# A two-layer hybrid decoder step on one core: a 64-byte gap behind the constants, earlier requests for the ada blocks, and a normalisation whose rest is subtracted tile by tile

## The chip, the cores and the metric

The kernel runs on one core of a Trainium2 chip. The metric is device time in microseconds (us) for one execution; lower is better. Engines are named as in the profile: PE is TensorE (PEld its weight loads), DVE is VectorE, ACT is ScalarE, POOL is GpSimd, SP is SyncE, which issues all the DMAs of this kernel.

## What is computed

One inference step of a trunk of two layers, for a prompt of 512 tokens and 8 samples of 8 tokens, which is 576 tokens (T) of 1024 channels. Each layer, in float32:

```
sh1, sc1, g1, sh2, sc2, g2 = split(silu(c) @ w_ada + b_ada, 6)
h = x * (1 + sc1) + sh1
mix, k, v, conv = mixer(h)          # w_in, dilated attention, conv module, merge, w_out
x = LayerNorm(alpha * x + g1 * mix)
h = x * (1 + sc2) + sh2
x = LayerNorm(alpha * x + g2 * ((silu(h @ w_gate) * (h @ w_up)) @ w_down))
```

The new keys and values and the conv states are outputs too.

## The kernel before, in words

Activations lie channel-major in SBUF: x is 8 tiles of 128 channels by 576 tokens. Each engine has its own program, written out by hand; semaphores order them.

**Units.** Weights come in units of 128 output channels by 1024 inputs (SP, line 350, into one of two `w_raw` buffers). ACT rounds a unit to `w_hi` (line 508) and DVE takes the remainder `w_lo` (line 839), three buffers each. PE forms hi*hi + lo*hi + hi*lo for each of 8 channel tiles and two halves of 288 tokens, so a unit is 48 matmuls (line 1231). A layer has 20 units for w_in (0 to 19), 8 for w_out (20 to 27), 44 for gate and up, 24 for w_down.

**Unit pairs after a normalisation.** The first two units of w_in and of gate/up are done by `products_by_tile` (line 1251): as each channel tile of h arrives, PE does the six matmuls of the first unit for it, and six of the second unit for the tile that is LAG behind.

**ada blocks.** w_ada comes in 96 blocks of 1 MB. Blocks 16 to 23 are used inside units 22 to 25 of layer 0, two in a unit, before its channel tiles 3 and 7 (`ada_quad`, line 1340, four matmuls, recorded as eight), out of a ring of two buffers. SP asks for block n only once block n-2 has been used (line 357). SP works strictly in the order written; `around(l, u)` stands behind the fetch of unit u. In it the ada blocks stand ahead of the two stores `k_d` and `v_d` (lines 428, 431; 1.18 MB each), which belong to u = 25.

**Normalisation.** There are four: in each layer one behind w_out (q = 0) and one behind w_down (q = 1). The mean of tiles 0 to 4 is subtracted early. Behind the last unit: DVE adds the last residual; PE sums the rest of the mean (line 1260); ACT loads the Sqrt table (558), copies the rows of squares (560), squares the last tile (549) and the rest (563); PE turns rows into columns (1324, 1327); DVE subtracts the rest from tiles (`take_rest`, 959), reduces the columns (969) and takes the reciprocal (972) after ACT's root (565); PE spreads the result over PSUM (1281, recorded as twelve matmuls); DVE multiplies each tile by it (`normalise`, 985). After the first three normalisations ACT scales each tile (520), rounds it to `h_hi` (527), and DVE takes `h_lo` (858), on which `products_by_tile` waits; DVE's program runs two normalised tiles ahead of `h_lo`. After the fourth ACT scales each tile (540) and SP stores y.

Of the kernel before, what the change touches and what calls it, by code (L numbers as in the profile page):

```python
# [21 lines left out]
P = 128  # L22
# [20 lines left out]
ALPHA = (2 * DEPTH) ** 0.25  # L43
SCALE = HD ** -0.5
NEG = -1e30
LAG = 4
HF = 3
MOST = 3.0e38
M_ORDER = [*range(4, 8), *range(4)]
# [53 lines left out]
for _k in range(QB - 1):  # L103
# [17 lines left out]
           c_norm=CT, cz=CT, z_sq=CT, z_rows=1, z_rows_sb=1, p_sq=1, t_sq=1, o_rows=1, o_rows_sb=1, m_var=1, m_sd=1, m_rcol=1,  # L121
           m_spread=2, rstdc_sb=1, m_f=CT, m_hi=2 * CT, m_lo=2 * CT,
           ln_sum=4, ln_mean=2, ln_cent=2 * NCEN, ln_acc=2, ln_sq=2 * NCEN, ln_rows=2, ln_rows_sb=2, ln_rest=2,
           ln_cols=2, ln_var=2, ln_sd=2, ln_rcol=2, ln_rstd=2, a_hi=FT, a_lo=FT, vec_used=1)


class Steps:
# [31 lines left out]
def trunk(nc, xT, cT, ba_d, w_ada, w_mix, w_dn, kc_d, vc_d, st_d, vec_d, rope_d, eye_d, mp_d, msc_d, msn_d,  # L159
          y_d, k_d, v_d, cp_d, cs_d):  # L160
    with ExitStack() as ctx:
        def sb(name, shape, dt=F32, where=ctx):
            return where.enter_context(nc.sbuf_tensor("sb_" + name, shape, dt))
# [22 lines left out]
        w_lo = sb("w_lo", [P, NW, UNIT], F32R)  # L186
        eye = sb("eye", [P, P])
        ones = sb("ones", [P, P])
        rope = sb("rope", [P, 2, T])
        mp = sb("mp", [P, SEQ])  # L190
        msc = sb("msc", [P, PAST])
# [146 lines left out]
        def _(sp):  # L338
# [39 lines left out]
            def around(l, u):  # L378

                if u == 1:  # L380
                    need(sp, s["vec_used"], l)
                    sp.dma_start(vec[:], vec_d[l]).then_inc(s["vec_in"], 16)
                if l == 0:
                    for n, at in IN_QUADS.items():
                        if u == (max(3, IN_QUADS[n - 2] + 5) if n - 2 in IN_QUADS else 1):
                            fetch_quad(n)
                    for n in range(GU_QUAD0, QUADS):
                        at = GU0 + 2 * (n - GU_QUAD0) if n < DN_QUAD0 else DN0 + 3 * ((n - DN_QUAD0) // 2) + 2 * ((n - DN_QUAD0) % 2)
                        if u == at + 2:
                            fetch_quad(n)  # L390
                if u == 4:
                    sp.wait_ge(s["w_used"], l * UL + 1)
                    sp.dma_start(uS[:, :, :, 0:HIST], st_d[l]).then_inc(s["hist"], 16)
                if u == 13:
                    sp.wait_ge(z_free[1], z_taken(l, Z_IN, CT - 1))
                    sp.wait_ge(s["hist_zero"], l + 1)
                    sp.dma_start(cp_d[l], uP[:, :, SEQ:SEQ + HIST]).then_inc(s["cv_st"], 16)
                    sp.wait_ge(s["hist"], nth(l, "hist", 15))
                    sp.dma_start(cs_d[l], uS[:, :, :, NT:NT + HIST]).then_inc(s["cv_st"], 16)
                if u == (14 if l == 0 else 5):  # L400
                    sp.wait_ge(s["ada_used"], 16 if l == 0 else QUADS)
                    fetch_cache(l, "k", 0)
                if u == QKV0 + 9:
                    sp.wait_ge(s["ss_ps"], nth(l, "ss_ps", 0))
                    fetch_cache(l, "v", 0)
                if u == QKV0 + 12:
                    sp.wait_ge(s["os_ps"], nth(l, "os_ps", 0))
                    fetch_cache(l, "k", 1)
                if u == QKV0 + 15:
                    sp.wait_ge(s["ss_ps"], nth(l, "ss_ps", 1))  # L410
                    fetch_cache(l, "v", 1)
                    sp.wait_ge(s["w_used"], l * UL + N_IN)
                    fetch_cache(l, "k", 2)
                    fetch_cache(l, "k", 3)
                if u == QKV0 + 16:
                    sp.wait_ge(s["os_ps"], nth(l, "os_ps", 1))
                    fetch_cache(l, "v", 2)
                    sp.wait_ge(s["ss_ps"], nth(l, "ss_ps", 2))
                    fetch_cache(l, "v", 3)
                if l == 0:  # L420
                    for n, (at, _) in OUT_QUADS.items():
                        if u == at + (2 if n < 18 else 3):
                            if n < 18:
                                sp.wait_ge(s["os_ps"], nth(0, "os_ps", 2))
                            fetch_quad(n)
                if u == QKV0 + 17:
                    sp.wait_ge(s["rope_done"], nth(l, "rope_done", 2 * CT - 1))
                    sp.dma_start(k_d[l], qk[:, CT:2 * CT, :]).then_inc(s["k_st"], 16)
                    for j in range(2):
                        sp.wait_ge(z_free[j], z_taken(l, Z_IN, N_IN // 2 - 1))  # L430
                    sp.dma_start(v_d[l], vT[:]).then_inc(s["v_st"], 16)
# [67 lines left out]
        def _(act):  # L499
# [55 lines left out]

            def norm_last(l, q):

                nc.scalar.preload_act_table(ACT.Sqrt)
                act.wait_ge(s["ln_rows"], nth(l, "ln_rows", q))
                nc.scalar.activation(halves(rows[0:3 * GW, :]), ROWS_PS[0:3 * GW], ACT.Copy).then_inc(s["ln_rows_sb"], 1)  # L560
                squares(l, q, NCEN - 1)
                act.wait_ge(s["ln_sum"], nth(l, "ln_sum", 2 * q + 1))
                nc.scalar.activation(halves(rows[3 * GW:P, :]), REST_PS[3 * GW:P], ACT.Square, scale=1.0 / D).then_inc(s["ln_rest"], 1)
                act.wait_ge(s["ln_var"], nth(l, "ln_var", q))
                nc.scalar.activation(sd_col, var_col, ACT.Sqrt, bias=eps[0:TW]).then_inc(s["ln_sd"], 1)
# [87 lines left out]
            for l in range(DEPTH):  # L653
# [121 lines left out]
                for m in range(KT - 1):  # L775
                    u = OUT0 + m
                    computed(l, u)
                    if l == 0 and u + 1 == 26:
                        ada_copy(2)
                    split(l, u + 3)  # L780
                    if m == KM:

                        act.wait_ge(s["k_st"], 16 * (l + 1))
                        act.wait_ge(s["v_st"], 16 * (l + 1))
                        norm_first(l, 0)
                    if m == KT - 2:
                        for c in range(NCEN - 1):
                            squares(l, 0, c)
                split(l, OUT0 + KT + 2)
                norm_last(l, 0)  # L790
                modulate(l, 1)
# [16 lines left out]
                for m in range(KT):  # L808
                    for r in range(3):
                        u = DN0 + 3 * m + r  # L810
                        if r == 0 and l == 0 and m == 1:
                            ada_copy(5)
                        if r == 2:
                            if m == KM:
                                norm_first(l, 1)
                            if m == KT - 2:
                                for c in range(NCEN - 1):
                                    squares(l, 1, c)
                        if u < UL - 1:
                            split(l, u + 3)  # L820
                norm_last(l, 1)
# [6 lines left out]
        def _(dve):  # L828
# [132 lines left out]
            def norm_last(l, q):  # L961

                for j in range(2):
                    dve.wait_ge(z_free[j], z_taken(l, (Z_OUT, Z_DN)[q], KT // 2 - 1))
                dve.wait_ge(s["ln_rest"], nth(l, "ln_rest", q))
                for k in range(3):
                    take_rest(l, q, k)
                dve.wait_ge(s["ln_cols"], nth(l, "ln_cols", q))
                nc.vector.tensor_reduce(var_col, COLS_PS.rearrange("p (c j) -> p j c", c=2), mybir.AxisListType.X, ALU.add)\
                    .then_inc(s["ln_var"], 1)  # L970
                dve.wait_ge(s["ln_sd"], nth(l, "ln_sd", q))
                nc.vector.reciprocal(rstd_col, sd_col).then_inc(s["ln_rcol"], 1)
                for k in range(3, KT - 1):
                    take_rest(l, q, k)

            def normalise(l, q, k):
                if k == 0:
                    dve.wait_ge(s["ln_rstd"], nth(l, "ln_rstd", q))
                    st.wait(st.n)
                if k == KT - 1:  # L980
                    dve.wait_ge(s["ln_sq"], nth(l, "ln_sq", NCEN * q + NCEN - 1))
                    take_rest(l, q, k)
                    st.wait(st.n)
                xk = halves(x[:, k, :])
                nc.vector.tensor_tensor(xk, xk, RSTD_PS, ALU.mult).then_inc(s["x_hat"], 1)

            def ada_bias(sec):

# [231 lines left out]
        def _(pe):  # L1220
# [53 lines left out]
                    ins = nc.tensor.matmul(dst[:, j:j + 1], rows_sb[:, j * TW:(j + 1) * TW], ones[:, 0:1], start=True, stop=True)  # L1274
                return ins

            def spread(dst, col):

                for j in range(TG):
                    half, o = divmod(j * TW, H)  # L1280
                    ins = nc.tensor.matmul(dst[:, half, o:o + TW], col[:, j:j + 1].to_broadcast([TW, P]), eye[0:TW, 0:TW],  # L1281
                                           start=True, stop=True)
                return ins
# [34 lines left out]
            def norm_last(l, q):  # L1318
# [8 lines left out]
                    ins = nc.tensor.matmul(COLS_PS[:, TG + j:TG + j + 1], rows[:, j * TW:(j + 1) * TW], row_pick, start=True, stop=True)  # L1327
                ins.then_inc(s["ln_cols"], 1)
                pe.wait_ge(s["ln_rcol"], nth(l, "ln_rcol", q))
                spread(RSTD_PS, rstd_col).then_inc(s["ln_rstd"], 1)  # L1330

            def ada_quad(n):

# [470 lines left out]
```

## Time and profile before

| what | us |
|---|---|
| median of 3 runs | 1585.09 (1582.12 to 2086.45) |
| the profiled execution | 1584.71 |
| its span, first to last instruction | 1582.8 |
| PE busy in the span | 1500.7 |
| DVE busy | 766.4 |
| ACT busy | 548.7 |

The span is what the trace shows; the profiled execution's time is 1.9 us more, for what lies around it. Matmuls are pipelined and overlap in their records, so PE's pace is read from the times between starts and not from its busy share. An idle time in square brackets behind a row of the timeline is that of the engine just before the row, with what ended it.

### The profile page before, as it was taken

The page shows a single profiled execution, that of the slowest core. Times are in us where ns is not written, and L with a number is a line of the kernel's source. Part 1 is how long each engine was busy: PE and PEld are TensorE (multiplying, and loading weights), DVE is VectorE, ACT ScalarE, POOL GpSimd, SP SyncE. Part 2 cuts the span into 40 slices and gives each one's busy share as a digit, 9 for nine tenths or more (in the row PEclk, how much of TensorE's full clock was granted, in tenths as well). Part 3 has the DMA queues.
Part 4 walks back from the last instruction along what each step waited for, and adds up shares of the span by engine and source line. Part 5 has one row for each costly group of instructions (what it writes and reads, how often), then busy time and mean ns, then how long its engine had stood idle before and what let it go on. Part 6 is the DMA issues. An engine that isn't in the chain of part 4 may idle for free.

```text
span 1582.8 us, 26321 instructions
## 1 busy us (share of the span) xinstructions
PE 1500.7 (95%) x11456; PEld 1359.0 (86%) x11456; DVE 766.4 (48%) x1207; ACT 548.7 (35%) x862; POOL 84.9 (5%) x104
## 2 busy tenths in 40 slices
PE   5999988889999999999989999889899999999996
PEld 2887766779999999899979977569799999999995
DVE  1798974364232232322347989846633333332233
ACT  3425566134222222211235255662533222221122
POOL 1000000111000000001001000002100000000100
PEclk7999999989999999999999999989899999999998
DMA  9576244623334433332214542514022222222221
GB/s 382 179 170 175 94 188 173 261 79 147 137 143 160 160 149 143 134 112 78 80 56 133 80 123 98 225 78 140 29 92 81 80 81 88 86 77 84 77 71 61
DMA packets 59523, 197.16 MB, mean 125 GB/s; under 512 B 22544, under 2 KB 22928, under 8 KB 48400
## 3 DMA queue, kind: packets, MB, share of 16 engines
q1 hardware_dynamic: 59408, 195.48, 37.1%
q8 instruction: 91, 1.49, 0.4%
q14 instruction: 24, 0.20, 0.0%
HBM read 187.27 MB, written 8.18 MB: 123 GB/s over the span
## 4 chain that ended last, share of the span: by engine, by line
PE 83%; DVE 6%; ACT 5%; DMA 2%; issue 2%; SPq 0%; POOL 0%; ACTq 0%; DVEq 0%; POOLq 0%
PE ps L1231 68%; PE ps L1340 2%; PE ps L1251 2%; PE ps L1609 2%; DVE sb_y L875 2%; DMA sb_x<-xT 1%; PE ps L1373 1%; ACT sb_E L589 1%; PE ps L1260 1%; PE ps L1281 1%; PE ps L1484 1%; DVE sb_h L858 1%; PE ps L1407 1%; DMA sb_ring<-w_ada 1%; PE ps L1396 1%
## 5 line engine op out<-in xcount | busy, mean ns | idle before, releaser
L1231 PE MATMUL ps<-sb_h,sb_w_hi 128*128 128x288 f32 x4224 | 770.2, 299 | 0.0
L1231 PEld LDWEIGHTS ps<-sb_h,sb_w_hi 128*128 128x128 f32 x4224 | 627.5, 189 | 51.8 <-issue 50.8
L1231 PE MATMUL ps<-sb_h,sb_w_lo 128*128 128x288 f32 x2112 | 451.8, 296 | 0.0
L839 DVE TENSOR_TENSOR sb_w_lo<-sb_w_raw,sb_w_hi 128x1024 fp32r<-128x1024 f32 x192 | 234.8, 1224 | 357.5 <-ACT sb_w_hi L508 357.1
L1231 PEld LDWEIGHTS ps<-sb_h,sb_w_lo 128*128 128x128 f32 x2112 | 340.1, 189 | 0.0
L508 ACT ACTIVATE sb_w_hi<-sb_w_raw 128x1024 fp32r<-128x1024 f32 x192 | 202.1, 1053 | 320.1 <-PE ps L1231 305.8
L875 DVE SCALAR_TENSOR_TENSOR sb_y<-sb_uP,sb_vec,sb_y 128x512 f32<-128x512 f32 x240 | 164.9, 744 | 0.5
L1231 PE MATMUL ps<-sb_a_hi,sb_w_hi 128*128 128x288 f32 x704 | 151.8, 297 | 0.0
L1231 PE MATMUL ps<-sb_a_lo,sb_w_hi 128*128 128x288 f32 x704 | 150.8, 296 | 0.0
L1231 PE MATMUL ps<-sb_a_hi,sb_w_lo 128*128 128x288 f32 x704 | 150.7, 296 | 0.0
L803 ACT ACTIVATE sb_a_hi<-sb_af 128x576 fp32r<-128x576 f32 x44 | 30.2, 686 | 266.7 <-DVE sb_af L1185 266.7
L1185 DVE TENSOR_TENSOR sb_af<-ps,sb_gate 128x576 f32<-128x576 f32 x44 | 33.3, 758 | 177.0 <-PE ps L1231 174.7
L1231 PEld LDWEIGHTS ps<-sb_a_hi,sb_w_hi 128*128 128x128 f32 x704 | 113.4, 189 | 3.7 <-issue 3.5
L1231 PEld LDWEIGHTS ps<-sb_a_lo,sb_w_hi 128*128 128x128 f32 x704 | 113.4, 189 | 0.0
L1231 PEld LDWEIGHTS ps<-sb_a_hi,sb_w_lo 128*128 128x128 f32 x704 | 113.4, 189 | 0.0
L798 ACT ACTIVATE sb_gate<-ps 128x576 f32<-128x576 f32 x44 | 28.7, 652 | 159.1 <-PE ps L1231 155.7
L1251 PE MATMUL ps<-sb_h,sb_w_hi 128*128 128x288 f32 x256 | 54.5, 329 | 17.9 <-DVE sb_h L858 17.3
L1251 PEld LDWEIGHTS ps<-sb_h,sb_w_hi 128*128 128x128 f32 x256 | 43.4, 213 | 22.0 <-issue 18.3
L1187 DVE TENSOR_TENSOR sb_a_lo<-sb_af,sb_a_hi 128x576 fp32r<-128x576 f32 x44 | 33.4, 758 | 33.1 <-ACT sb_a_hi L803 33.1
L580 ACT ACTIVATE sb_E<-sb_E,sb_small 128x128 f32<-128x128 f32 (+3 forms) x64 | 35.4, 554 | 38.9 <-DVE sb_small L1019 38.6
L1340 PE MATMUL ps<-sb_ring,sb_c_in 128*32 128x512 f32 x320 | 42.9, 608 | 4.1 <-DMA sb_ring<-w_ada 4.1
L1396 PE MATMUL ps<-sb_eye,sb_E 128*128 128x128 f32 x160 | 28.5, 281 | 13.4 <-ACT sb_PT L598 8.1
(192 smaller groups left out, 1208.6 us busy)
## 6 DMA issues: line engine op xcount, KB each, us to landing
sb_w_raw<-w_mix SPq DMA_DIRECT2D x144, 512.0 KB, 3.5
sb_ring<-w_ada SPq DMA_DIRECT2D x40, 1024.0 KB, 5.8
sb_w_raw<-w_dn SPq DMA_DIRECT2D x32, 512.0 KB, 3.5
sb_ring<-vc_d SPq DMA_DIRECT2D x12, 1024.0 KB, 8.5
sb_big<-w_ada SPq DMA_DIRECT2D x8, 1024.0 KB, 11.9
sb_ring<-kc_d SPq DMA_DIRECT2D x8, 1024.0 KB, 7.5
sb_w_raw<-w_dn SPq DMA_DIRECT2D x16, 384.0 KB, 3.2
sb_cache_a<-kc_d SPq DMA_DIRECT2D x4, 1024.0 KB, 7.4
```

Source lines behind the costliest of these rows:

```text
L508: nc.scalar.activation(w_hi[:, g % NW, :], w_raw[:, g % NR, :], ACT.Copy).then_inc(s["hi_ready"], 1)
L580: nc.scalar.activation(blk, blk, ACT.Exp, bias=nm8[p % 2][:, c:c + 1], scale=-1.0, accum_out=den8[p % 2][:, c:c + 1]).then_inc(s["exp_read ...
L803: nc.scalar.activation(a_hi[:, i], af[:], ACT.Copy).then_inc(s["a_hi"], 1)
L839: nc.vector.tensor_tensor(w_lo[:, g % NW, :], w_raw[:, g % NR, :], w_hi[:, g % NW, :].bitcast(F32), ALU.subtract)\
L875: ins = nc.vector.scalar_tensor_tensor(out=yp, in0=up, scalar=tap, in1=yp, op0=ALU.mult, op1=ALU.add)
L1185: nc.vector.tensor_tensor(halves(af[:]), Z[1], halves(gate[:]), ALU.mult).then_inc(z_free[1], 1)
L1187: nc.vector.tensor_tensor(a_lo[:, i], af[:], a_hi[:, i].bitcast(F32), ALU.subtract).then_inc(s["a_lo"], 1)
L1231: ins = nc.tensor.matmul(z[:, i], a[:, g % NW, w], b[:, k0 + k, i * H:(i + 1) * H], start=first and k == 0 and t == 0, stop=last and k == ...
L1251: ins = nc.tensor.matmul(Z[u][:, i], a[:, j, w], b[:, k, i * H:(i + 1) * H], start=n == 0 and t == 0, stop=n == KT - 1 and t == 2)
L1340: ins = nc.tensor.matmul(ps[j * GW:(j + 1) * GW, ADA_BANK[k], :], c_in[:, kt, :], buf[:, j * 512:(j + 1) * 512], start=kt == 0, stop=kt == ...
L1396: ins = nc.tensor.transpose(ps[:, 6 + j % 2, (q - k) * P:(q - k + 1) * P], E[:, e, o:o + P], eye[:])
L1609: ins = nc.tensor.matmul(Z[u][:, i], a[:, j, w], b[:, k, i * H:(i + 1) * H], start=n == 0 and t == 0, stop=n == KT - 1 and t == 2)
```

## The change

One float tile of 64 bytes per partition that nothing uses is allocated behind `ones`, so that all tiles allocated later start 64 bytes further on. LAG goes from 4 to 2. Blocks 18 to 23 are written one unit earlier in SP's program. In the normalisation ACT's table load moves up, ahead of the last units' work, and the last square comes before the copy of the rows; DVE subtracts the rest from two tiles before the columns (three before), from two more after the reciprocal (four before), and from tiles 4 to 7 each just before its own multiplication (tile 7 alone before); the spread signals after each half, and tile 0 is multiplied in halves.

```diff
-LAG = 4
+LAG = 2
@@ allocations
         ones = sb("ones", [P, P])
+        sb("gap", [P, 16])
@@ around (SP)
-                        if u == at + (2 if n < 18 else 3):
+                        if u == at + 2:
@@ norm_last (ACT); the table load now behind squares() at m == KT - 2
-                nc.scalar.preload_act_table(ACT.Sqrt)
+                squares(l, q, NCEN - 1)
                 act.wait_ge(s["ln_rows"], nth(l, "ln_rows", q))
                 nc.scalar.activation(halves(rows[0:3 * GW, :]), ...)
-                squares(l, q, NCEN - 1)
@@ norm_last (DVE)
-                for k in range(3):
+                for k in range(2):
                     take_rest(l, q, k)
 ...
-                for k in range(3, KT - 1):
+                for k in range(2, 4):
                     take_rest(l, q, k)
             def normalise(l, q, k):
+                if k >= 4:
+                    if k == KT - 1:
+                        dve.wait_ge(s["ln_sq"], ...)
+                    take_rest(l, q, k)
+                st.wait(st.n)
+                xk = halves(x[:, k, :])
                 if k == 0:
-                    dve.wait_ge(s["ln_rstd"], nth(l, "ln_rstd", q))
+                    dve.wait_ge(s["ln_rstd"], nth(l, "ln_rstd", 2 * q))
+                    st.of(nc.vector.tensor_tensor(xk[:, 0], xk[:, 0], RSTD_PS[:, 0], ALU.mult))
+                    dve.wait_ge(s["ln_rstd"], nth(l, "ln_rstd", 2 * q + 1))
+                    ins = nc.vector.tensor_tensor(xk[:, 1], xk[:, 1], RSTD_PS[:, 1], ALU.mult)
                     st.wait(st.n)
 ...
@@ norm_last (PE)
-                spread(RSTD_PS, rstd_col).then_inc(s["ln_rstd"], 1)
+                for i in range(2):
+                    spread(RSTD_PS, rstd_col, range(i * TG // 2, (i + 1) * TG // 2)).then_inc(s["ln_rstd"], 1)
```

The order of the instructions shows two places. DVE, the normalisation behind w_down of layer 0, before; line 959 is the rest, 985 the multiplication, 858 `h_lo`:

```order
427 L959 SCALAR_TENSOR_TENSOR sb_x<-ps,sb_x 128x576 x3
428 L969 TENSOR_REDUCE sb_cols<-ps 96x6
429 L972 RECIPROCAL sb_cols<-sb_cols 96x6
430 L959 SCALAR_TENSOR_TENSOR sb_x<-ps,sb_x 128x576 x4
431 L985 TENSOR_TENSOR sb_x<-sb_x,ps 128x576 x3
432 L858 TENSOR_TENSOR sb_h<-sb_hf,sb_h 128x576
```

The same place in the changed kernel, up to the multiplication of tile 5 (961 is now the rest, 987, 989 and 992 the multiplication, 860 `h_lo`):

```order
432 L961 SCALAR_TENSOR_TENSOR sb_x<-ps,sb_x 128x576 x2
433 L971 TENSOR_REDUCE sb_cols<-ps 96x6
434 L974 RECIPROCAL sb_cols<-sb_cols 96x6
435 L961 SCALAR_TENSOR_TENSOR sb_x<-ps,sb_x 128x576 x2
436 L987 TENSOR_TENSOR sb_x<-sb_x,ps 128x288
437 L989 TENSOR_TENSOR sb_x<-sb_x,ps 128x288
438 L992 TENSOR_TENSOR sb_x<-sb_x,ps 128x576 x2
439 L860 TENSOR_TENSOR sb_h<-sb_hf,sb_h 128x576
440 L992 TENSOR_TENSOR sb_x<-sb_x,ps 128x576
441 L860 TENSOR_TENSOR sb_h<-sb_hf,sb_h 128x576
442 L961 SCALAR_TENSOR_TENSOR sb_x<-ps,sb_x 128x576
443 L992 TENSOR_TENSOR sb_x<-sb_x,ps 128x576
```

Three rests have moved from ahead of the first multiplication to between the multiplications of tiles 4, 5 and 6. SP, units 24 to 27 of layer 0, before; `sb_ring<-w_ada x2` are blocks 16 and 17, then 18 and 19, and so on, and the two stores belong to unit 25:

```order
43 L357 DMA sb_ring<-w_ada 128x2048 x2
44 L350 DMA sb_w_raw<-w_mix 128x1024
45 L428 DMA k_d<-sb_qk 128x2304
46 L431 DMA v_d<-sb_vT 128x2304
47 L350 DMA sb_w_raw<-w_mix 128x1024
48 L357 DMA sb_ring<-w_ada 128x2048 x2
49 L350 DMA sb_w_raw<-w_mix 128x1024
```

The same place in the changed kernel:

```order
43 L358 DMA sb_ring<-w_ada 128x2048 x2
44 L351 DMA sb_w_raw<-w_mix 128x1024
45 L358 DMA sb_ring<-w_ada 128x2048 x2
46 L429 DMA k_d<-sb_qk 128x2304
47 L432 DMA v_d<-sb_vT 128x2304
48 L351 DMA sb_w_raw<-w_mix 128x1024
49 L358 DMA sb_ring<-w_ada 128x2048 x2
```

Blocks 18 and 19 have moved ahead of the two stores and of unit 26's weights.

## Rows read from the trace of the kernel before

**Rows 1.** The page, busy time and share of the span by engine.
```profile
PE 1500.7 (95%) x11456; PEld 1359.0 (86%) x11456; DVE 766.4 (48%) x1207; ACT 548.7 (35%) x862; POOL 84.9 (5%) x104
```
**Rows 2.** Timeline, second normalisation of layer 0: start, us, engine, line, operation.
```profile
819.22 0.68 ACT L549 ACTIVATE sb_sq_h<-sb_x 128x576 f32<-128x576 f32 x1 [2.35 <-DVE sb_x L940]
...
820.32 1.10 PE L1324 MATMUL ps<-sb_small,sb_sq_h 128*96 128x1 f32 x12
...
820.52 0.64 ACT L563 ACTIVATE sb_rows<-ps 32x576 f32<-32x576 f32 x1 [0.61 <-PE ps L1260]
...
821.28 1.16 PE L1327 MATMUL ps<-sb_small,sb_rows 128*96 128x1 f32 x12
821.30 2.08 DVE L959 SCALAR_TENSOR_TENSOR sb_x<-ps,sb_x 128x576 f32<-128x576 f32 x3 [1.34 <-ACT sb_rows L563]
823.31 0.16 DVE L969 TENSOR_REDUCE sb_cols<-ps 96x6 f32<-96x12 f32 x1
...
824.07 2.87 PE L1281 MATMUL ps<-sb_eye,sb_cols 96*128 96x96 f32 x12 [1.63 <-DVE sb_cols L972]
...
826.98 2.08 DVE L985 TENSOR_TENSOR sb_x<-sb_x,ps 128x576 f32<-128x576 f32 x3 [0.34 <-PE ps L1281]
...
829.33 0.76 DVE L858 TENSOR_TENSOR sb_h<-sb_hf,sb_h 128x576 fp32r<-128x576 f32 x1 [0.27 <-ACT sb_h L527]
...
836.46 0.74 DVE L959 SCALAR_TENSOR_TENSOR sb_x<-ps,sb_x 128x576 f32<-128x576 f32 x1
...
837.24 0.75 DVE L985 TENSOR_TENSOR sb_x<-sb_x,ps 128x576 f32<-128x576 f32 x1
837.91 0.75 DVE L858 TENSOR_TENSOR sb_h<-sb_hf,sb_h 128x576 fp32r<-128x576 f32 x1
```
**Rows 3.** Chain that ended last, in order of time: the pair's last stretch on PE.
```profile
838.72 8.25 PE ps L1251 x60
```
**Rows 4.** Timeline, first normalisation of layer 1.
```profile
1118.42 1.28 ACT L558 ACT_TABLE_LOAD   x1
...
1119.36 1.21 PE L1260 MATMUL ps<-sb_x,sb_ones 128*128 128x288 f32 x4
...
1119.71 0.65 ACT L560 ACTIVATE sb_rows<-ps 96x576 f32<-96x576 f32 x1
...
1120.95 0.64 ACT L563 ACTIVATE sb_rows<-ps 32x576 f32<-32x576 f32 x1
```
**Rows 5.** Timeline, last normalisation, at the end of the program.
```profile
1572.46 4.74 DVE L985 TENSOR_TENSOR sb_x<-sb_x,ps 128x576 f32<-128x576 f32 x7 [0.34 <-PE ps L1281]
1573.25 6.31 ACT L540 ACTIVATE sb_x<-sb_x,sb_pend 128x576 f32<-128x576 f32 x8 [3.98 <-DVE sb_x L985]
```
**Rows 6.** Timeline, SP's issues and PE around the ada blocks of layer 0.
```profile
282.92 0.43 SPq L428 DMA_DIRECT2D k_d<-sb_qk  x1
...
286.10 4.56 SPq L357 DMA_DIRECT2D sb_ring<-w_ada  x2
...
297.77 1.37 PE L1340 MATMUL ps<-sb_ring,sb_c_in 128*32 128x512 f32 x8 [4.12 <-DMA sb_ring<-w_ada]
```
**Rows 7.** Blocks 16 to 24: us from issue to landing.
```profile
DMA to landing us min/median/max: 4.8/5.6/11.6
```
**Rows 8.** Chain that ended last: 24 matmuls behind block 18, and behind block 19.
```profile
299.14 4.59 PE ps L1231 x24
303.73 0.99 PE ps L1340 x8
304.73 3.38 PE ps L1231 x24
```
**Rows 9.** Stretches: us, busy by engine, granted PE clock, DMA share, GB/s.
```profile
296.00:298.00 2.00, 0.23 (x4) 0.16 (x8) 0.00 (x0) 0.00 (x0) 0.00 (x0) 1.00 1.01 424
...
300.00:302.00 2.00, 2.00 (x11) 2.00 (x11) 0.00 (x0) 0.00 (x0) 0.00 (x0) 0.55 0.87 258
```
**Rows 10.** Stretches of two unit pairs: first of layer 0 whole, then a beginning.
```profile
34.10:49.80 15.70, 15.49 (x97) 14.97 (x98) 7.71 (x9) 12.02 (x17) 5.87 (x13) 0.84 0.84 280
...
830.20:834.20 4.00, 3.81 (x14) 3.50 (x15) 3.44 (x6) 3.78 (x6) 1.78 (x5) 0.50 0.00 0
```
**Rows 11.** Groups of instructions: line, operation, count, busy us, mean ns.
```profile
L1268 PE MATMUL ps<-sb_sqc,sb_ones 128*32 128x288 f32 x64 | 4.7, 411 | 2.1 <-ACT sb_sqc L733 2.1
...
L1268 PE MATMUL ps<-sb_sqm,sb_ones 128*32 128x288 f32 x32 | 2.8, 418 | 0.0
```

More of the change, by code:

```diff
@@ L123 @@
            ln_sum=4, ln_mean=2, ln_cent=2 * NCEN, ln_acc=2, ln_sq=2 * NCEN, ln_rows=2, ln_rows_sb=2, ln_rest=2,
-           ln_cols=2, ln_var=2, ln_sd=2, ln_rcol=2, ln_rstd=2, a_hi=FT, a_lo=FT, vec_used=1)
+           ln_cols=2, ln_var=2, ln_sd=2, ln_rcol=2, ln_rstd=4, a_hi=FT, a_lo=FT, vec_used=1)
 class Steps:
@@ L788, in _ @@
                             squares(l, 0, c)
+                        nc.scalar.preload_act_table(ACT.Sqrt)
                 split(l, OUT0 + KT + 2)
@@ L818, in _ @@
                                     squares(l, 1, c)
+                                nc.scalar.preload_act_table(ACT.Sqrt)
                         if u < UL - 1:
@@ L972, in norm_last @@
                 nc.vector.reciprocal(rstd_col, sd_col).then_inc(s["ln_rcol"], 1)
-                for k in range(3, KT - 1):
+                for k in range(2, 4):
                     take_rest(l, q, k)
             def normalise(l, q, k):
+                if k >= 4:
+                    if k == KT - 1:
+                        dve.wait_ge(s["ln_sq"], nth(l, "ln_sq", NCEN * q + NCEN - 1))
+                    take_rest(l, q, k)
+                st.wait(st.n)
+                xk = halves(x[:, k, :])
                 if k == 0:
-                    dve.wait_ge(s["ln_rstd"], nth(l, "ln_rstd", q))
+                    dve.wait_ge(s["ln_rstd"], nth(l, "ln_rstd", 2 * q))
+                    st.of(nc.vector.tensor_tensor(xk[:, 0], xk[:, 0], RSTD_PS[:, 0], ALU.mult))
+                    dve.wait_ge(s["ln_rstd"], nth(l, "ln_rstd", 2 * q + 1))
+                    ins = nc.vector.tensor_tensor(xk[:, 1], xk[:, 1], RSTD_PS[:, 1], ALU.mult)
                     st.wait(st.n)
[L980 to L985, printed above, removed]
+                else:
+                    ins = nc.vector.tensor_tensor(xk, xk, RSTD_PS, ALU.mult)
+                ins.then_inc(s["x_hat"], 1)
             def ada_bias(sec):
@@ L1275, in token_cols, with spread @@
                 return ins
-            def spread(dst, col):
-                for j in range(TG):
+            def spread(dst, col, groups=range(TG)):
+                for j in groups:
                     half, o = divmod(j * TW, H)
```

## The prediction

> **What bounds the kernel now.** I read the page first: PE is busy 1500.7 of 1582.8 us [rows 1], so only places where PE stands still, or waits behind others, can give anything back. The chain that ended last and the timeline then show which places the change touches: the stretch around ada block 18, four normalisations, three unit pairs behind them, and the unit pair at the start. Everything else keeps its instructions and its order. All sums are made against the profiled execution, 1584.71 us; the three runs were 1582.12, 1585.09 and one far off, so it lies on the median within half a microsecond.
>
> **The normalisation ahead of a pair.** In layer 0 behind w_down [rows 2], DVE starts three rests at 821.30 and reduces the columns only at 823.31, when the third is through, though PE's last column matmul ends at 821.28 + 1.16 = 822.44. With two rests (0.67 us a piece, since three take 2.08 and one 0.74) DVE is free at about 822.7. But ACT's copy of the rows, 0.65 us [rows 4], now follows the last square, which starts at 819.22 and takes 0.68 [rows 2]; it ends at about 820.5, and the column matmuls that started at 820.32 slip by 0.3, to an end at 822.75. So the reduction comes at about 822.9: 0.4 earlier. Then the spread, 2.87 us, is unchanged, but behind it only half of tile 0 has to be multiplied, some 0.45 instead of 0.72: 0.27 more. Tile 0 is normalised 0.67 earlier.
>
> Where the table load lies on the path more is won. In layer 1 behind w_out it runs from 1118.42 to 1119.70, the copy follows, and ACT starts on the rest at 1120.95, though PE's sum for it ended at 1119.36 + 1.21 = 1120.57 [rows 4]. With the load done earlier, beside the last units' matmuls, where ACT waits for PE anyway, the rest starts at 1120.6; this and the third rest give 0.8, with the half 1.05. Were that cover gone, the load would cost its 1.28. The same normalisation in layer 0 I put between the two, at 0.85.
>
> **The price of it.** Three rests move in between the multiplications of tiles 4, 5 and 6. A rest and the wait for it cost 0.78 there, as tile 7's do before (836.46 to 837.24) [rows 2]: 2.34 us in all. From the start of `h_lo` of tile 0 (829.33) to the end of tile 5's (837.91 + 0.75 = 838.66) DVE has twelve instructions, eleven at 0.67 and that rest, 8.15 us of 9.33. So 1.2 are free; I let 1.0 of them take new work, since the waits for tiles 0 and 1 stay. Tile 5 then comes 1.34 later, less the earlier start.
>
> **LAG.** Before, when tile 5 arrives, PE still has 60 matmuls to do, and does them without a stop in 8.25 us [rows 3]: 0.1375 each. With LAG 2 two tiles of the second unit, 12 matmuls, have been done by then in time that PE spent waiting, and 48 are left: 6.60, so 1.65 less. Behind w_down that makes -1.65 + 1.34 - 0.67 = -0.98; with starts of 1.05 and 0.85 the other two give -1.36 and -1.16. Together **-3.5**. The bounds: -5.5, if all the free time takes rests and PE's low clock at a pair's start (granted 0.50, 1.2 GHz [rows 10]) ends sooner; 0, if DVE's free time takes none of them. The second units' weights are no new wait: both are split before the residual of the last tile.
>
> At the program's start PE is busy in 15.49 of the 15.70 us of its pair [rows 10]; LAG can only win what is idle: **-0.2**.
>
> **The end.** Behind the last normalisation no matmul follows. DVE multiplies eight tiles, seven from 1572.46 on [rows 5], ACT scales them in 6.31, and y goes out behind the last. The three rests are on the path whole: +2.34, less some 0.45 of earlier start (between 0.3 and 0.67), **+1.9**. ACT hides none of it: eight scalings at 0.79 end at 1579.56, no later than DVE's last tile allows.
>
> **The ada blocks.** Block 18 is asked for at 286.10 [rows 6] and lands 11.6 us later, where others take 4.8 to 5.6 [rows 7]. PE stops for it from 293.65 to 297.77. Behind that its clock is granted 0.55, near 1.2 GHz instead of 2.4 [rows 9], and the 24 matmuls that follow take 4.59 against 3.38, the block's own 1.37 against 0.99 [rows 6, 8]. The stop costs 4.12 + 1.21 + 0.38 = 5.7.
>
> The earlier place in SP's program does not make the request much earlier: it waits until block 16 has been used, and that is what released it at 286.1. What changes is what lies ahead of it. Block 18 now goes ahead of the stores (issued from 282.92 before) and lands at about 291.7, in time for 293.65. Block 19 needs block 17 used, 290.25 (the second request of the row of 4.56 us); SP stands still until then, and the stores, unit 26's weights and block 20 stand behind it. Block 19 lands at 295.9, needed at 293.65 + 0.99 + 3.38 = 298.0. Block 20 is wanted at 302.4. Ahead of it from 290.25 on are block 19 (1.05 MB), the stores (2.36) and the weights (0.52), with itself 4.98 MB, at 424 GB/s [rows 9] 11.7 us. Before, the four pieces from the first store to block 18, 3.93 MB, took from 282.92 to 297.7, 14.8 us, 5.5 more than the rate alone; if half to three quarters of that stays, block 20 lands between 304.7 and 306.1. So the stop moves from block 18 to block 20, 302.4 to about 305.6: 3.2 us. I charge the same 1.6 for the clock. **-0.9**, between +0.5 (a stop of 4.6) and -5.7 (none). Unit 26's weights come later too, but are needed only two units on; ACT's wait for the stores, ahead of the mean at unit 25, lies behind their landing.
>
> By the Trainium skill ("DMA: Bandwidth & Descriptors", section "Queues, rings and completion order") each DMA engine takes the descriptors of a ring in order, so that block 20 cannot pass the stores; the 11.6 against 5.6 us agree [rows 7]. By that rule the stop moves, as summed; if a block could pass, the stretch would give 5.7.
>
> **The gap.** No instruction is added. It shifts `h`, `a_hi` and `ring` from a multiple of 128 bytes to 64 past one. The nearest rows are two equal sums on PE, over `sqc` (on a multiple of 128) and `sqm` (96 past one): 411 and 418 ns [rows 11]. The whole difference, 1.7%, would be 25 us of PE's 1500.7 [rows 1], in either direction; but these two stand in different surroundings, so I take **0**.
>
> **Sum.** -3.5 - 0.2 + 1.9 - 0.9 = -2.7: 1582.0 us.
>
> **Rivals.**
> 1. *The stop at the ada blocks goes and does not come back.* For it: block 19 and the stores could run as fast as the 424 GB/s of the row, and then block 20 lands at about 302.8 and PE barely stops. Against it: the 14.8 us for 3.93 MB. It gives 5.7 instead of 0.9: 1577.2.
> 2. *The pairs lose what they win (slower).* With LAG 2 PE does twelve matmuls for a tile, 1.65 us, and tiles 4 to 7 come 2.1 apart (0.67 + 0.67 + 0.78 on DVE), so it stands still between them; if the clock stays at 1.2 GHz for that, each matmul costs 0.13 more (14 took 3.81 us [rows 10], 0.27 each). For it: the row with 0.55 behind a stop. Against it: before, PE also had holes in these stretches and rose. From 21 more slow matmuls, over the three pairs together, the 2.7 are gone; 24 more in each pair cost 9.4: 1591. The Trainium skill ("TensorE: Matmul & The Clock Gate", section "What's actually happening") has it that throttled is the default and activity releases it, which would go this way; the rise within the pairs [rows 10] shows that sparse work was enough.
> 3. *DVE sets the pace, the free time takes nothing:* each tile from 5 on comes 2.34 later less its start, the pairs give 0.5, and the other three terms sum to +0.8: 1585.0. For it: DVE is busy most of that stretch; against it: the 1.2 us counted above.
> 4. *The addresses matter:* 1557 or 1609.
>
> **How the numbers follow.** Forecast (1579.5 to 1584.5) 0.52; rival 1 0.17; rival 2 0.12; rival 3 0.13; rival 4 0.06, halved by sign. The range goes from 1575.5, rival 1 with the better bound of the pairs at half, to 1588, rival 2 with half its price; outside lie rival 4 and half of rival 2, 0.12. About 2%, 31.7 us, is what a measurement of this kernel can tell from no change; only the addresses reach that far, from 2.1% of PE's time on: faster 0.02, slower 0.03, within 0.95.
>
> **What would show it.** No stop at block 18; a stop of about 3 us at block 20, with a granted clock near 0.5 behind it. The reduction of the columns directly behind PE's, not behind a rest. On PE some 48 matmuls without a stop at the end of a pair. The last multiplication 1.9 us later, counted from the last spread. The prediction is wrong if matmuls of equal shape change their pace, if PE waits for `h_lo` of tile 7, or if the y stores no longer follow ACT.

## The result, and the profile after the change

| | before | after |
|---|---|---|
| median | 1584.09 (6 runs, 1581.73 to 1585.09 and one far off at 2086.45) | 1575.12 (6 runs, 1572.60 to 1577.15) |
| ratio, without the run far off | | 0.9944, 95% interval 0.9934 to 0.9955 |
| profiled execution, span | 1582.8 | 1570.8 |
| PE busy | 1500.7 [rows 1] | 1489.6 |

The change takes 9.0 us off, 0.56%, where 2.7 had been forecast: within 2%, but just outside the range of 1575.5 to 1588.0. The profiled execution of after is the fastest of its six, so its trace shows some 3 us more than the medians.

The page of after, busy time of PE:

```profile
PE 1489.6 (95%) x11456; PEld 1348.6 (86%) x11456; DVE 767.1 (49%) x1211; ACT 549.4 (35%) x862; POOL 85.0 (5%) x104
```

PE does the same 11456 matmuls and is busy 11 us less; DVE and ACT are as busy as before. So something happened to the matmuls themselves. The chain that ended last shows it where they follow one another without a stop (start, us, engine, line, count). Before:

```profile
846.97 57.61 PE ps L1231 x432
...
1147.40 369.60 PE ps L1231 x2772
...
1517.97 25.59 PE ps L1231 x192
```

After (line 1231 is now 1239):

```profile
838.03 57.12 PE ps L1239 x432
...
1136.95 366.52 PE ps L1239 x2772
...
1504.44 25.39 PE ps L1239 x192
```

369.60 / 2772 = 133.33 ns a matmul before, 366.52 / 2772 = 132.22 after: 0.83% less, at the full clock in both (granted 1.00 over these stretches). The program has 8448 + 384 + 192 = 9024 matmuls of this shape (lines 1231, 1251 and 1609 before; a third of the units of w_down have 36 and not 48); 1.11 ns on each would be 10.0 us if all ran at the full clock and PE never waited for others.

Where the 12.0 us of the span went, in us, from the starts of the same matmuls in the two traces:

| stretch | before | after | difference |
|---|---|---|---|
| up to the last unit of w_out, layer 0 | 340.72 | 338.24 | -2.48 |
| normalisation and unit pair behind it | 30.32 | 28.21 | -2.11 |
| gate, up, w_down of layer 0 | 446.62 | 443.81 | -2.81 |
| normalisation and pair behind it | 29.01 | 27.47 | -1.54 |
| w_in, attention, w_out of layer 1 | 270.27 | 271.35 | +1.08 |
| normalisation and pair behind it | 30.16 | 27.58 | -2.58 |
| gate, up, w_down of layer 1 | 416.04 | 412.66 | -3.38 |
| last normalisation to the end | 19.68 | 21.50 | +1.82 |

Of the first row's 2.48, 1.2 are there by 279 us, before the ada blocks; between executions that start differs by as much.

### The profile page after: what moved, and what is told of

Read it like the earlier page. It is cut to its first block, busy times and chain, and to the rows that moved or that the text cites. A ratio compares the mean times of both kernels' runs of the same rounds, so it can differ in the third digit from the quotient of the medians.

```text
span 1570.8 us, 26329 instructions
## 1 busy us (share of the span) xinstructions
PE 1489.6 (95%) x11456; PEld 1348.6 (86%) x11456; DVE 767.1 (49%) x1211; ACT 549.4 (35%) x862; POOL 85.0 (5%) x104
## 4 chain that ended last, share of the span: by engine, by line
PE 84%; DVE 8%; ACT 4%; DMA 2%; issue 2%; SPq 0%; POOL 0%; DVEq 0%; ACTq 0%; POOLq 0%
PE ps L1239 69%; PE ps L1349 3%; PE ps L1259 2%; PE ps L1618 2%; DVE sb_y L877 2%; PE ps L1382 1%; DMA sb_x<-xT 1%; ACT sb_E L589 1%; PE ps L1268 1%; DVE sb_x L992 1%; DVE sb_x L961 1%; DVE sb_h L860 1%; PE ps L1493 1%; PE ps L1289 1%; PE ps L1321 1%
```

## Experiments: is it the gap?

**The gap alone.**

```diff
         ones = sb("ones", [P, P])
+        sb("gap", [P, 16])
```

> The kernel before with one line more: 64 bytes left free behind ones, so that everything laid out behind it (h, a_hi, a_lo, the ring of raw blocks) starts 64 bytes past a multiple of 128 bytes. Theory A (where the moving operand starts sets the pace of the matmuls): the long chain row of equal matmuls goes from 133.3 ns a matmul to 132.2 ns, as in the changed kernel, and over about 9000 such matmuls the time falls by 8 to 10 us, to 1575 to 1576 us. Theory B (the pace went with the shorter lead of the blocks, LAG 2 in place of 4, because a split of weights meets the matmuls at another moment): nothing moves here, 133.3 ns and 1584 us. Theory C (the pace differs from run to run): the time stays within 1 us of the kernel before on the same chip, whatever the pace in one profile is.

Ratio 0.9946 (0.9930 to 0.9963), which is -8.5 us (-11.1 to -5.9), nearly the whole gain; the medians, 1576.91 for 1583.53, are 6.6 apart. The chain:

```profile
842.92 57.12 PE ps L1232 x432
...
1141.82 366.52 PE ps L1232 x2772
```

**The change without its gap.**

```diff
-        sb("gap", [P, 16])
```

> The changed kernel without its gap: LAG 2, the ada blocks one unit earlier and the new order in the normalisation stay. Theory A (the gap sets the pace): 133.3 ns a matmul as before, and 1581 to 1582 us, which is what the prediction's sum gives with the gap at nothing. Theory B (LAG sets the pace): 132.2 ns a matmul and 1575 us, as the changed kernel with its gap.

Ratio 0.9990 (0.9980 to 1.0000), so -1.6 us (-3.2 to 0.0). The pace is the old one:

```profile
1140.85 369.60 PE ps L1238 x2772
```

Theory A holds so far: the gap sets the pace, neither LAG nor the execution does; whether it is the streamed operand's own start that counts comes next. The prediction's -2.7 for all the rest lies between -3.2 and 0.0.

## Experiments: which address counts?

**h moves by 64 bytes.** `pend` takes 64 bytes a partition; laid out behind h it leaves the weights and the blocks behind h where they were. Only `vec`, `c_in`, `small`, the ring and what shares h's place move with h.

```diff
-        pend = sb("pend", [P, 2, KT])     # ahead of vec
...
         h = sb("h", [P, KT, 2, T], F32R)
+        pend = sb("pend", [P, 2, KT])
```

> The kernel before with one small constant (pend, 64 bytes a partition) laid out behind h and not in front of it: h starts 64 bytes lower, so 64 past a multiple of 128 bytes, while a_hi, a_lo and the weights stay where they were. Theory M (the start of the moving operand sets the pace): matmuls that stream h at 132.2 ns, those that stream a_hi and a_lo still at 133.3 ns, in the same run; about 6600 of 9000 such matmuls gain, so about 1578 us. Theory D (the gap worked through something else that moved, such as the blocks behind h): all at 133.3 ns, 1584 us.

Ratio 0.9973 (0.9954 to 0.9992). The chain has both paces in one run: 432 matmuls over h, then a stretch that is mostly h, then 192 over a_hi and a_lo:

```profile
844.92 57.12 PE ps L1231 x432
...
1142.69 367.35 PE ps L1231 x2772
1511.01 25.58 PE ps L1231 x192
```

57.12 / 432 is 132.2 ns, 25.58 / 192 is 133.2: the operand that moved changed its pace, the others did not. Of the 2772, the 42 units of gate and up, 2016 matmuls, stream h and 756 stream a_hi and a_lo; 2016 at 132.22 and 756 at 133.33 are 367.35, as measured.

**The weights move by 64 bytes, the streamed operands stay.** The constants laid out between the weights and `pend` move too.

```diff
+        pend = sb("pend", [P, 2, KT])
         w_hi = sb("w_hi", [P, NW, UNIT], F32R)
...
-        pend = sb("pend", [P, 2, KT])     # ahead of vec
```

> The kernel before with pend laid out in front of w_hi: the weights w_hi and w_lo start 64 bytes later, h, a_hi and a_lo stay where they were. Theory M (the start of the moving operand alone): nothing moves, 133.3 ns a matmul, 1584 us. Theory W (what counts is where the moving operand starts against the weights, which are loaded meanwhile): the same 64 bytes between them as with the gap, so 132.2 ns and 1576 us.

Ratio 0.9963 (0.9944 to 0.9982). h, a_hi and a_lo stand where they did, and yet:

```profile
843.15 57.12 PE ps L1231 x432
...
1141.85 366.52 PE ps L1231 x2772
1509.34 25.38 PE ps L1231 x192
```

Theory M falls, theory W holds: what counts is where the streamed operand starts against the weights.

**Everything moves by 64 bytes.**

```diff
+        sb("gap", [P, 16])
         x = sb("x", [P, KT, T])
```

> The kernel before with the 64 bytes left free in front of everything: weights, h, a_hi and a_lo all start 64 bytes later, so their distance from one another is as before. Theory W (the distance of the moving operand's start from the weights' start, within 128 bytes, sets the pace): 133.3 ns a matmul, 1584 us. Theory E (it is enough that either of the two is off a multiple of 128 bytes): 132.2 ns, 1576 us.

Ratio 1.0001 (0.9991 to 1.0011), and the old pace; so being off a multiple of 128 bytes is not what helps:

```profile
845.61 57.61 PE ps L1232 x432
...
1146.04 369.60 PE ps L1232 x2772
```

**h moves by 384 bytes, to a multiple of 512.**

```diff
-        b_ada = sb("b_ada", [P, SECTIONS, KT])     # ahead of pend
...
         h = sb("h", [P, KT, 2, T], F32R)
+        b_ada = sb("b_ada", [P, SECTIONS, KT])
```

> The kernel before with b_ada (384 bytes a partition) laid out behind h: h starts 384 bytes lower, on a multiple of 512 bytes where it was 384 past one; a_hi, a_lo and the weights stay. Theory M128 (only the start within 128 bytes counts): h still at 133.3 ns a matmul, 1584 us. Theory M512 (the start within 256 or 512 bytes counts): the matmuls that stream h change their pace, to either side, those that stream a_hi and a_lo keep 133.3 ns.

Ratio 0.9999 (0.9988 to 1.0011); 432 matmuls over h took what they took before: 384 bytes, three times 128, change nothing. From tile to tile of one run, too, streamed operand and weights are other multiples of 128 bytes apart, so what is left of the distance within 128 bytes is what counts:

```profile
846.85 57.61 PE ps L1231 x432
```

**Other distances.** The gap's size in floats is 8, 4, 12 and 24 in place of 16.

```diff
-        sb("gap", [P, 16])
+        sb("gap", [P, 8])
```

> The kernel before with a gap of 32 bytes in place of 64 behind ones. If any start off a multiple of 128 bytes gives the pace of the gap: 132.2 ns a matmul and 1576 us. If it must be half of 64 or 128 bytes apart: 133.3 ns or another pace, no lower than 131 ns, the commonest single distance of before.

> The kernel before with a gap of 16 bytes: moving operands 16 bytes past the weights' phase. If only a distance of 64 gains (theory H, half of 128): 133.3 ns a matmul, 1584 us. If the distance matters by degree (theory G): a pace between 132.2 and 133.3, or one that is worse than both.

> The kernel before with a gap of 48 bytes. Theory H: 133.3 ns a matmul, 1584 us. Theory G: between 133.3 (the 32 bytes) and 132.2 (the 64 bytes), 1576 to 1584 us.

> The kernel before with a gap of 96 bytes, which is as far from the next multiple of 128 as 32 bytes are from the last. Theory H, and a theory by which the distance counts the same to both sides: 133.3 ns a matmul as with 32 bytes, 1584 us. If only the direction counts (moving operand more than half behind): 132.2 ns, 1576 us.

The chains of 32, 16, 48 and 96 bytes, in this order:

```profile
1145.35 369.60 PE ps L1232 x2772
```
```profile
1148.17 369.60 PE ps L1232 x2772
```
```profile
1141.27 366.52 PE ps L1232 x2772
```
```profile
1144.57 369.60 PE ps L1232 x2772
```

| streamed operand's start minus the weights', within 128 bytes | ns a matmul | ratio of times |
|---|---|---|
| 0 (before) | 133.33 | 1 |
| 16 | 133.33 | 1.0010 (0.9994 to 1.0026) |
| 32 | 133.33 | 1.0006 (0.9990 to 1.0023) |
| 48 | 132.22 | 0.9949 (0.9926 to 0.9971) |
| 64, by the gap | 132.22 | 0.9946 (0.9930 to 0.9963) |
| 64, by the weights | 132.22 | 0.9963 (0.9944 to 0.9982) |
| 96 | 133.33 | 1.0007 (0.9995 to 1.0018) |

There are two paces among these and nothing between; 48 gains as much as 64, so theory H (64 alone) is too narrow and theory G (by degree) is wrong. Where the gain begins between 32 and 48 and where it ends between 64 and 96 was not tried. The paces are means. In the traces' steady stretches the single starts follow patterns: at 0, three come about 131 ns behind the one before and the fourth 140; at 16 and 32, 135 and 132 alternate; at 96 they lie between 129 and 139; at 48 and 64, between 130 and 135. So the slow pace is the same mean by three patterns, not one delay on each matmul.

## Experiments: the other parts

**The ada blocks alone.**

```diff
-                        if u == at + (2 if n < 18 else 3):
+                        if u == at + 2:
```

> The kernel before with the request of the ada blocks from 18 on one unit earlier, alone. By the prediction's term the stop of 4.1 us ahead of block 18 goes, one of about 3 us ahead of block 20 comes, and 24 matmuls behind it lose about 1 us to the clock: -0.9 us, so about 1583.2 us. Rival 1 (no stop is left at all): -5 to -6 us, so 1578 to 1579 us. By the changed kernel's trace, in which the stream of matmuls is 2.4 us early behind block 20 of which 1.2 us came before: about -1.2 us.

Ratio 1.0001 (0.9988 to 1.0015): nothing that can be measured. The stop moved from block 18 to block 20 here as in the change, but was longer (timeline of PE, with its idle time, then the chain):

```profile
304.69 1.93 PE L1340 MATMUL ps<-sb_ring,sb_c_in 128*32 128x512 f32 x8 [3.52 <-DMA sb_ring<-w_ada]
```
```profile
306.63 5.26 PE ps L1231 x24
```

Stop 3.52, slow block 1.93 - 0.99, slow matmuls 5.26 - 3.38: 6.3, against 5.7 before [rows 6, 8]. In the traces of the change, of the change without its gap and of the better version below, the same edit brings the stream 1.3, 1.5 and 1.3 us forward.

**The normalisation alone.** The edits of `norm_last`, `normalise` and the spread; LAG 4, no gap, ada blocks as before.

> The kernel before with the new normalisation alone (table loaded behind the squares, two halves of the spread signalled apart, rest subtracted tile by tile from the fifth on); no gap, LAG 4, ada blocks as before. By the prediction's terms: -1.2, -1.0 and -1.4 us in front of the three unit pairs, a little at the start pair, and +1.9 us at the end, where no matmuls hide the tiles: -1.5 to -2 us in sum, 1582 to 1582.5 us, with the pace of the matmuls at 133.3 ns. If the reordering itself changed the pace: 132.2 ns and 1574 us.

Ratio 1.0020 (1.0009 to 1.0031): slower by 3.2 us, where 1.5 to 2 us faster had been expected. PE's waits in the first pair of layer 0 (sum, times, longest):

```profile
PE ps L1258 <- DVE sb_h L859: 5.7, 5, 3.0
```

Before, and then with LAG 2 alone (the next run), the same wait:

```profile
PE ps L1251 <- DVE sb_h L858: 3.9, 3, 3.3
```
```profile
PE ps L1251 <- DVE sb_h L858: 3.5, 2, 3.3
```

The longest is the wait for tile 0. The pair starts 1.1 us sooner (12.81 us behind the start of the last product, for 13.90), and then PE stands still 2.7 us for tiles that the inserted rests have made late; before it stood 0.6.

**LAG alone.**

```diff
-LAG = 4
+LAG = 2
```

> The kernel before with LAG 2 in place of 4, alone: in the unit pairs PE does twelve matmuls a tile from the third tile on, not from the fifth. The old normalisation hands over its first tile later and the others quickly, and PE stood 0.7 to 1.0 us for the fifth tile and 0.5 us for the seventh. Theory 1 (the shorter lag takes these stops away by itself): about 1 us less in each of the three pairs, 1581 us. Theory 2 (the lag pays only together with the new normalisation, which without it lost what it won): within 1 us of 1584. Sum of parts: the changed kernel without its gap is at 1582 to 1583, and the normalisation alone is at +3, so with the ada blocks at 0 the lag has to give 4 to 5 us in the new normalisation's company.

Ratio 0.9978 (0.9965 to 0.9991): -3.5 us, theory 1. The interval in us from the first to the last matmul of the three pairs, all without the gap (the new normalisation with LAG 2 is the change without its gap):

| | LAG 4 | LAG 2 |
|---|---|---|
| old normalisation | 16.42, 16.43, 16.43 | 15.69, 15.51, 14.98 |
| new normalisation | 17.79, 18.85, 17.80 | 16.19, 16.18, 16.18 |

The new normalisation costs a pair 0.5 to 1.2 us with LAG 2 and 1.4 to 2.4 with LAG 4, and starts it 1.1 to 2.4 us earlier in five of six (the sixth, behind w_down with LAG 2, 0.1 later). Summed over the three pairs of these single traces that is 1.7 us gained with LAG 2 and 0.7 lost with LAG 4. The times without the gap do not show the gain: 0.9990 for the change without its gap, whose end is 1.5 us longer than before, against 0.9978 for LAG 2 alone.

**Gap and LAG 2 alone.** Does the normalisation add anything to them?

```diff
+        sb("gap", [P, 16])
-LAG = 4
+LAG = 2
```

> The kernel before with the gap of 64 bytes and LAG 2 alone; the old normalisation and the ada blocks as before. If the parts add up: 0.9946 by 0.9978 of 1584, which is 1572 us, 3 us under the whole change and level with the version whose end is mended; then the new normalisation and the ada blocks add nothing in sum. If the new normalisation pays in the company of LAG 2 (its pairs ran 1 to 1.5 us shorter than those of LAG 2 alone): 1574 to 1576 us, and the mended version stays in front.

Ratio 0.9965 (0.9953 to 0.9978), median 1577.61: the second theory by its side, if 1.6 us above its numbers. The parts do not add up: beside the gap alone (0.9946) LAG 2 shows no gain. The whole change (0.9944, 0.9934 to 0.9955) is ahead of these two, though the intervals touch; the version below (0.9925) is clear of them. Its pairs are shorter than those of the gap alone (normalisation and pair 28.86, 27.70, 28.52 against 30.09, 28.97, 29.86), 3.8 us in sum, but w_in to w_out of layer 1 took 272.05 against 269.03.

**A better version.** The changed kernel with the rests of the very last normalisation subtracted early again.

```diff
@@ norm_last (DVE)
-                for k in range(2, 4):
+                for k in range(2, KT - 1 if (l, q) == (DEPTH - 1, 1) else 4):
                     take_rest(l, q, k)
@@ normalise
-                    take_rest(l, q, k)
+                    if k == KT - 1 or (l, q) != (DEPTH - 1, 1):
+                        take_rest(l, q, k)
```

> The changed kernel, but in the very last normalisation, behind which no matmul follows, the rests of tiles 4 to 6 are subtracted while PE makes the reciprocal deviation, as in the kernel before. By the prediction's term for the end and the changed kernel's trace, 1.9 to 2.0 us come back: 1573 us. If the end is set by the output's transfer or by ACT: nothing, 1575 us.

Ratio 0.9925 (0.9912 to 0.9938), median 1572.55: below the change's 0.9944, though the intervals touch and the two were measured apart. The timeline of DVE at the end, here and then in the changed kernel:

```profile
1560.72 4.07 DVE L993 TENSOR_TENSOR sb_x<-sb_x,ps 128x576 f32<-128x576 f32 x6
```
```profile
1558.79 2.07 DVE L992 TENSOR_TENSOR sb_x<-sb_x,ps 128x576 f32<-128x576 f32 x3
1560.79 0.75 DVE L961 SCALAR_TENSOR_TENSOR sb_x<-ps,sb_x 128x576 f32<-128x576 f32 x1
1561.57 0.75 DVE L992 TENSOR_TENSOR sb_x<-sb_x,ps 128x576 f32<-128x576 f32 x1
```

Six multiplications in a row, where the change has three and then a rest before each. From the last product to the end it takes 19.52 us, against 21.50 in the change and 19.68 before.

**And LAG 1.**

```diff
-LAG = 2
+LAG = 1
```

> The same with LAG 1 in place of 2. In the unit pairs of the changed kernel PE still stands 0.6 us for the third tile and 0.4 for the last; with a lag of one tile it has six matmuls more to do early. If PE stands for tiles there: a few tenths less in each of three pairs, 1572 us. If the twelve matmuls at a tile then wait for the second unit's weights, or the sum of matmuls and not the tiles is the bound: 1573 us.

Ratio 0.9920 (0.9905 to 0.9936), median 1571.63. The three pairs take 15.35 each, against 16.15 in the version above, but the median is only 0.9 us lower and the intervals overlap: clearly faster than before, by the medians 3.5 us faster than the change (the intervals touch), not shown to be faster than LAG 2. What the pairs won went in part to layer 1 (below).

## Why the prediction missed

**The gap: the step that failed.** The prediction took it at 0 and gave its rival 4, "the addresses matter", 0.06 with 25 us to either side. They matter, and the gap is worth -8.5 us; the first of the prediction's own signs of being wrong, that matmuls of equal shape change their pace, came true. Two things went wrong. The row that it was judged by had nothing to do with addresses: sums over `sqc` and `sqm`, 411 and 418 ns [rows 11]. The gap moves both, and the groups of after read

```profile
L1276 PE MATMUL ps<-sb_sqc,sb_ones 128*32 128x288 f32 x64 | 4.7, 411 | 2.1 <-ACT sb_sqc L733 2.1
...
L1276 PE MATMUL ps<-sb_sqm,sb_ones 128*32 128x288 f32 x32 | 2.8, 418 | 0.0
```

to the nanosecond the same. And a cost with a bound of 25 us to either side, nine times the sum of all other terms, was left out of the range but for a small chance: 0.83% on 9024 matmuls decides more here than every wait counted elsewhere. With the sign open, the range had to reach at least some way to both sides. As it stands, its ends do not follow from what they are said to be: rival 1 with half of the pairs' better bound is 1576.2 and not 1575.5, rival 2 with half its price 1586.7 and not 1588. The measured time lies outside by either.

**The normalisations and pairs: right mechanism, sizes off.** Forecast -1.16, -0.98 and -1.36; measured -2.11, -1.54 and -2.58. Single traces vary by some tenths here: in the run of the ada edit alone, which changes nothing in these stretches, they are 0.40, 0.00 and 0.25 shorter than before. The pair itself came out as summed: -1.65 + 1.34 = -0.31, measured 16.42 to 16.15. By the table above the terms are there one by one in two of the three pairs (+1.37 for the normalisation with LAG 4, -1.60 and -1.62 from there to LAG 2); behind w_down both are larger (+2.42, -2.67). The chain of after has the 48 matmuls at the end that the prediction asked for, in 6.61 us for 6.60:

```profile
360.13 6.61 PE ps L1259 x48
```

What was mis-sized is the earlier start of tile 0: forecast 0.85, 0.67 and 1.05, measured 1.84, 1.26 and 2.30. Multiplying half a tile gave 0.30 for 0.27. The reduction of the columns came 1.03, 0.58 and 0.93 earlier, where 0.58, 0.40 and 0.78 had been counted. The rest is the spread, which the prediction held at 2.87 us, "unchanged". In the chains it takes 2.89 before, and after, behind w_out of layer 1:

```profile
1115.14 0.31 ACT sb_cols L565
...
1115.48 0.20 DVE sb_cols L974
...
1115.72 1.81 PE ps L1289 x12
```

2.38 and 2.50 in the other two. The stretches (us, busy by engine, granted clock), before and after, in that spread:

```profile
1124.50:1127.40 2.90, 2.88 (x12) 2.63 (x12) 2.57 (x4) 0.00 (x0) 0.00 (x0) 0.50 0.00 0
```
```profile
1115.72:1117.53 1.81, 1.79 (x12) 1.55 (x12) 1.69 (x3) 0.00 (x0) 0.00 (x0) 0.84 0.00 0
```

In the trace of before, PE's clock had fallen to 1.2 GHz by then; in that of after, part of the spread still runs at 2.4, which makes 1.1 us at this place. That this comes of the shorter wait in front is not shown, because the run of the gap alone, with the old normalisation and its waits, has it too (timeline of PE):

```profile
1119.22 1.80 PE L1282 MATMUL ps<-sb_eye,sb_cols 96*128 96x96 f32 x12 [1.26 <-DVE sb_cols L973]
```

Over the thirteen traces with the old normalisation this spread takes from 1.80 to 2.88 us, over the five with the new one from 1.58 to 1.88, so the new order may make the fast one likelier; behind w_out of layer 0 it is the other way round, 1.81 to 2.88 and 2.22 to 2.88. The earlier start of tile 0 varies as much: against before, it is 1.97 and 2.49 us behind the two w_out and 0.15 us too late behind w_down in the change without its gap, and 1.32, 0.87 and 2.50 in the better version. The sign that was asked for shows: the reduction of the columns follows PE's last column matmul by less than 0.05 us in all four normalisations.

**Rivals 2 and 3** did not come: the pairs rose to the full clock (granted 1.00 from 360.00 to 366.50 in the first), and DVE's free time took the rests. But the run of the normalisation alone shows how near the third was: with LAG 4 the pair behind w_down grew by 2.42 us, where rival 3 had each late tile 2.34 later.

**The ada blocks: right in kind, too small to be seen in the times.** No stop at block 18, one at block 20, as the chain and the timeline of after show:

```profile
293.47 10.54 DMA sb_ring<-w_ada
...
305.55 4.48 PE ps L1239 x24
```
```profile
304.06 1.49 PE L1349 MATMUL ps<-sb_ring,sb_c_in 128*32 128x512 f32 x8 [2.91 <-DMA sb_ring<-w_ada]
```

The stretch behind it had a granted clock of 0.50:

```profile
305.60:308.00 2.40, 2.40 (x10) 2.40 (x11) 0.00 (x0) 0.00 (x0) 0.00 (x0) 0.50 0.94 338
```

2.91 + 0.5 + 1.1 = 4.5 for 5.7, so -1.2 where -0.9 was forecast. Rival 1 fell. In the run of this edit alone it was +0.6, so the term is as large as its own variation. One row was misread: 5.6 us is the median of the blocks [rows 7], and not the most that the others took; block 19 took 9.9. The landings that were forecast do not hang on it.

**The end: right.** +1.9 forecast, +1.82 in the trace; the version above takes it back. The pair at the program's start, 96 matmuls, went from 15.47 us to 14.91, for a forecast of -0.2; but in the better version, which is the same there, it took 15.71, so this term is not shown.

**What nobody had summed: layer 1 gives some back.** Between the pair behind w_down of layer 0 and the normalisation behind w_out of layer 1 the stream of matmuls came 8.94 us early and left 7.86 early, though by the pace its 1248 long matmuls should have won 1.4 us more there. In w_in of layer 1 DVE does the convolution and the rotation of q and k beside the matmuls, and is full. Stretches before and after, ahead of the first score matmul:

```profile
860.00:904.00 44.00, 44.00 (x332) 44.00 (x331) 43.79 (x64) 13.79 (x16) 1.77 (x2) 1.00 0.25 78
```
```profile
850.00:896.00 46.00, 45.15 (x342) 44.91 (x340) 45.68 (x67) 14.62 (x18) 1.78 (x2) 1.00 0.27 84
```

Before, PE and DVE were both busy to the last; after, only DVE is. The timeline of after shows the rotation, and PE's wait for it:

```profile
895.68 0.76 DVE L1016 TENSOR_TENSOR sb_qk<-sb_zcos,sb_zswap 128x576 f32<-128x576 f32 x1
...
896.65 0.49 PE L1382 MATMUL ps<-sb_qk 64*128 64x128 f32 x4 [1.50 <-issue]
```

The rotation ends at 896.44 and PE goes on at 896.65; the profile names no releaser for that stop. In the version with LAG 1, which comes still earlier, the wait is longer, and again PE goes on 0.21 us behind the rotation's end:

```profile
896.14 0.49 PE L1383 MATMUL ps<-sb_qk 64*128 64x128 f32 x4 [2.47 <-issue]
```

So what faster matmuls and shorter pairs win in front of it is not paid in full there, which is probably one reason why the parts do not add up; no run tests it. How much it took in each run stays open: the same stretch of layer 1 took 272.1 us in the run of the ada edit alone, which changes nothing there, against 270.3 before.

## What to carry to other kernels

Treat the layout of SBUF as an edit with a price: where thousands of equal matmuls follow one another, time one such run per matmul, and try the streamed operand 64 bytes off the weights' phase within 128 bytes. When an edit's effect can't be read from any row, compare its bound with the rest of the sum before calling it nothing, and ask whether the row used as a bound would react to the edit at all. A reordering that makes late tiles later cost time alone and came out ahead, in the traces, only with the edit that gives PE other work while they are late, so forecast and run such edits together, and look for the engine that is just in time behind the gain. Before a difference between two traces is put down to an edit, look at the same step in the runs that leave it alone: the spread's 1.1 us look like an effect of the new order, and the run of the gap alone has them too.

## What the runs showed of the hardware

A matmul with 128x128 weights that streams 288 columns of fp32r, in a stream in which weights are loaded for every matmul, takes 133.33 ns on the mean at the full clock when the streamed operand and the weights start 0, 16, 32 or 96 bytes apart modulo 128, and 132.22 ns at 48 or 64. In the slow stretches behind the stops at the ada blocks (granted 0.50 after, 0.55 before [rows 9]) the starts are 240 ns apart in both kernels, so there the distance does not show. The difference of pace is not the other engines' doing: in the last run of matmuls before the change none of them works (the stretch with busy time by engine, before), and the starts there are 133.2 ns apart as elsewhere.

```profile
1547.00:1558.00 11.00, 11.00 (x85) 11.00 (x84) 0.00 (x0) 0.00 (x0) 0.00 (x0) 1.00 0.00 1
```

The sums over `sqc` and `sqm`, whose weights are one constant block, did not react.

The Trainium skill ("TensorE: Matmul & The Clock Gate", section "Step-by-step: what each phase is for") gives PE two independent SBUF read ports, one for the streamed operand and one for the weights, so that loading the next weights takes no read bandwidth from the running matmul. By that a shift of the weights alone should change nothing; here it changed 133.33 ns to 132.22, so in this stream the two reads do not behave as wholly independent, though the cost is under 1%. The runs show that the distance counts, not how it comes about.

The same twelve matmuls of the spread took 2.89 us at a granted 0.50 and 1.81 at 0.84. Which of the two they meet varies between executions of one order of work; what decides it the runs do not show.
